# Running the context half of a second block in turns between expert blocks, on one core

## The reference

```
first_block(x):                         # 256 tokens
    h += forgetting_attention(norm(h));  h += hier_moe(norm(h), layer 0)
    h += retention(norm(h));             h += hier_moe(norm(h), layer 1)
hier_moe: 32 experts, top 2 of 8 in one of 4 groups; (silu(a) * b) @ w_down[e], w_gu[e] 1024 x 1024, w_down[e] 512 x 1024
second_block(x, ctx):                   # 256 tokens each, modulated by c and c_ctx
    for each of 2 layers, the same weights for x and ctx:
        p = norm(.) @ w_in              # 1024 x 3088: q, k, v, o, gates, SGU and convolution inputs
        mix = [mlstm (both directions) | spatial gating | depthwise convolution, 31 taps]
        . += gate * (mix @ w_out)       # 1024 x 1024
        . += gate * (silu(n @ w_g) * (n @ w_u)) @ w_down   # 1024 x 5632, 2816 x 1024
```

## Time and profile before

| | us |
|---|---|
| median of three runs | 2858.34 |
| lowest and highest | 2840.27, 2858.52 |
| profiled execution, its time | 2852.59 |
| profiled execution, its span | 2850.8 |

### The profile page before, as it was taken

One profiled execution on the slowest core, in us unless ns is written; L12 is line 12 of the kernel. 1 busy time (PEld: TensorE's weight loads), 2 busy tenths in 40 slices (PEclk: granted clock), 3 DMA queues, 4 the chain that ended last, 5 costly groups with the idle time before them and its releaser, 6 DMA issues. The chain is left out here.

```text
span 2850.8 us, 38893 instructions
## 1 busy us (share of the span) xinstructions
PE 2325.0 (82%) x16840; PEld 1697.3 (60%) x16840; DVE 1020.5 (36%) x1836; ACT 699.5 (25%) x1179; POOL 6.5 (0%) x16
## 2 busy tenths in 40 slices
PE   6998676667779987766666579888999998896998
PEld 6856432323358876423232247676788786675998
DVE  4334410100046354301010166574533226636544
ACT  4422100000034331000000042233322225233442
POOL 0000000000000000000000000000000000000000
PEclk9987778778789998888787788988999999887999
DMA  6473899999965675999999722101232223312542
GB/s 242 158 250 112 336 369 409 386 409 393 409 228 186 214 273 211 382 407 377 409 384 408 288 81 64 55 1 59 89 103 89 82 82 97 99 34 91 189 157 82
DMA packets 239524, 619.65 MB, mean 217 GB/s; under 512 B 11664, under 2 KB 64912, under 8 KB 239216
## 3 DMA queue, kind: packets, MB, share of 16 engines
q1 hardware_dynamic: 238832, 615.56, 57.8%
q0 software_dynamic: 512, 1.48, 0.2%
HBM read 615.95 MB, written 1.05 MB: 216 GB/s over the span
## 5 line engine op out<-in xcount | busy, mean ns | idle before, releaser
L351 PE MATMUL bank<-xh,high 128*128 128x256 f32 (+2 forms) x1328 | 451.5, 340 | 53.6 <-DVE xl L461 35.2
L351 PE MATMUL bank<-xl,high 128*128 128x256 f32 (+2 forms) x1328 | 446.9, 336 | 0.0
L351 PE MATMUL bank<-xh,low 128*128 128x256 f32 (+2 forms) x1328 | 446.3, 336 | 0.0
L351 PEld LDWEIGHTS bank<-xh,high 128*128 128x128 f32 (+1 forms) x1328 | 258.6, 195 | 96.0 <-issue 42.2
L351 PEld LDWEIGHTS bank<-xh,low 128*128 128x128 f32 (+1 forms) x1328 | 258.6, 195 | 25.7 <-issue 1.7
L351 PEld LDWEIGHTS bank<-xl,high 128*128 128x128 f32 (+1 forms) x1328 | 258.9, 195 | 22.6 <-issue 0.5
L1093 DVE TENSOR_TENSOR hs<-hs,bank 64x256 f32<-64x256 f32 x64 | 27.0, 423 | 624.9 <-ACT hs L1088 624.8
L1088 ACT ACTIVATE hs<-bank 64x256 f32<-64x256 f32 x64 | 24.2, 377 | 831.7 <-PE bank L1076 831.7
L318 DVE TENSOR_TENSOR low<-ring__6,high 128x1024 fp32r<-128x1024 f32 (+1 forms) x81 | 94.6, 1174 | 157.2 <-ACT high L309 157.2
L318 DVE TENSOR_TENSOR low<-ring__7,high 128x1024 fp32r<-128x1024 f32 x78 | 95.0, 1224 | 135.0 <-ACT high L309 134.8
L318 DVE TENSOR_TENSOR low<-ring__8,high 128x1024 fp32r<-128x1024 f32 x75 | 91.0, 1224 | 115.9 <-ACT high L309 115.8
(11 more groups left out here) (512 smaller groups left out, 3842.2 us busy)
## 6 DMA issues: line engine op xcount, KB each, us to landing
ring__7<-in_expert_w_down SPq DMA_DIRECT2D x32, 1024.0 KB, 14.4
ring__49<-in_expert_w_gu SPq DMA_DIRECT2D x16, 1024.0 KB, 16.6
ring__50<-in_expert_w_gu SPq DMA_DIRECT2D x16, 1024.0 KB, 18.5
ring__51<-in_expert_w_gu SPq DMA_DIRECT2D x16, 1024.0 KB, 18.5
ring__52<-in_expert_w_gu SPq DMA_DIRECT2D x16, 1024.0 KB, 18.6
ring__53<-in_expert_w_down SPq DMA_DIRECT2D x16, 1024.0 KB, 11.9
ring__54<-in_expert_w_down SPq DMA_DIRECT2D x16, 1024.0 KB, 13.6
ring__8<-in_expert_w_gu SPq DMA_DIRECT2D x16, 1024.0 KB, 15.3
```

Source lines behind the costliest of these rows:

```text
L351: done = pe.matmul(out, a.bitcast(F32R), b.bitcast(F32R), start=kk == 0 and q == 0, stop=stop)
```

## The change

The context half of the second block leaves the tail. Its layer 0 mixer runs inside `moe(0)` (`context_mixer`), its layer 0 FFN and layer 1's keys, values, gates and states inside `moe(1)` (`context_ffn`). Each is a Python generator for every engine. `schedule` takes the next piece of it (a turn) three times in each of its 34 rounds: after `up`, after `across` and after `down`, so 102 turns. The mixer has 72 turns (2 for the norm, 26 projection items, 36 for the scan and what lies around it, 8 output items). The part in `moe(1)` has 105 (2, 44 + 24 FFN items, 2, 10 projection items, 23), and three of them come behind the last round. The tail works on x's 256 columns and begins its scan from saved `states[L]` and `last_m`.

The weights for the turns go through the same ring. One load (up to 1 MB) serves two turns, and is issued two turns ahead of the first. To make room in the on-chip memory, the ring has 6 slots in the expert stages in place of 12, 5 in `fox`, 4 in `ret`, and 8 in the tail in place of 3; GB is 4; three banks serve `prepare`, `across` and `down` in place of four, and the eighth is the turns' own (`Halves`), with one matmul of zeros to open each group. The tables `cos`, `sin` and `dec` (0.79 MB) leave the load of `vec` and come in `ret` by POOL's queue. In the tail DVE does 5 taps after an item.

The core of the diff:

```diff
-GB = 8
+GB = 4
-NSLOT = 12
+NSLOT = 10
+NMOE = 6
...
+            def sp_paced(self, sp):
+
+                ahead = len(self.pairs.items)
+                self.loads(sp, 0, ahead)
+                for it in self.items:
+                    self.loads(sp, it["at"] + ahead, it["at"] + ahead + 1)
+                    yield it
...
+            def act_paced(self, act):
+                ahead = len(self.pairs.items)
+                self.act_high(act, ahead)
+                for it in self.items:
+                    self.evict(act, "a", ev_a, it)
+                    self.act_high(act, it["at"] + ahead + 1)
+                    yield it
...
-        def moe(L, before, opened, early_name, x_ready):
-            room = Room(f"moe{L}", 12, before, opened)
+        def moe(L, before, opened, early_name, x_ready, beside):
+
+            room = Room(f"moe{L}", NMOE, before, opened)
+            room.keeps = MORE[0]
...
+                turns = side["sp"](sp)
+                run(schedule(none, none, up, none, down, none, turns))
+                run(turns)
...
-            def schedule(prepare, scatter, up, across, down, back):
+            def schedule(prepare, scatter, up, across, down, back, turns):
                 prepare(0)
                 for b in range(NE + 2):
                     if b < NE:
                         up(b)
                     if b == 0:
                         scatter(0)
-                    if b % GB == 5 and b // GB + 1 < NE // GB:
+                    next(turns, None)
+                    if b % GB == 2 and b // GB + 1 < NE // GB:
                         prepare(b // GB + 1)
                         scatter(b // GB + 1)
                     if 1 <= b <= NE:
                         across(b - 1)
+                    next(turns, None)
                     if b >= 2:
                         back(b - 2)
                     if 1 <= b <= NE:
                         down(b - 1)
+                    next(turns, None)
                     yield b
...
+            room = Room("ret", 4, before, opened)
...
+        def context_mixer(room, bk):
+            return mixer(0, 0, room, room.part, room, bk, [], 2, 256, 7, 1)[2]
+
+        def context_ffn(room, bk):
+
+            pairs = pair_buffers(room, 2)
+            _, x_done, xx, first = ffn(0, 0, room, bk, [], pairs, 256, lambda c: [])
+            st, get = room.part()
+            second = mixer(1, 0, get, None, room, bk, x_done(7), pairs, 256, 7, 1, x_ready=x_done, xx=xx)[2]
+            st.close()
+            return one_after_another(first, second)
+
+        def x_mixer(L, before, opened, early_in, x_ready):
+            room = Room(f"mix{L}", 8, before, opened)
+            early, x_done, s = mixer(L, 1, room, room.part, room, banks, opened, 4, 512, 5, 2, early_in, x_ready)
```

## The result

The changed kernel takes 2965.57 us, median of four runs (2957.31 to 2983.26); the kernel before takes 2856.24 beside it. The ratio is 1.0403, with a 95% interval of 1.0342 to 1.0465. The forecast was slower, by 2.0% (2913). The time lies inside the range, the direction is right and the forecast step is half of what came. In the profiled executions the spans are 2965.5 and 2850.8, so 114.7 us more, where my sum had 60.

A forecast was written before the change was run, and what follows sets the result against it. Expert stages were taken as bound by transfers and the tail by PE. Turns cost 464 us, the tail and earlier weights give back 404, so +60 on the profiled 2852.6 gives 2913 us, range 2750 to 3010.

The forecast's parts named there:

- What bounds the kernel: Whole kernel: expert stages set by transfers at 394 GB/s with PE some 9 us a block free; the tail the opposite.
- The walk's mechanism: Expert stages: expert loads queue behind late-freed turn slots, PE waits for down and fourth up quarters; two blocks take 47.0 us.
- The tail's -404: Tail: 404 us saved through 256-column FFN, mixers, scans, outputs and norms, and earlier first weights.
- `moe(1)`'s +293: `ret` and `moe(1)`: 293 us more, including 226 for 26.6 blocks at 8.5 each.
- `prepare`: Expert stages, gather for four blocks: half meets free time, so it adds 1.0 us per block.
- `moe(0)`'s +171: Stretch to the end of `moe(0)`: 171 us more, including 70 for taps and 57 for projection and output.
- the taps' 70: `moe(0)`, 14 turns (4.7 blocks): DVE's gate steps or taps behind `low` add 6.4 per block, 70 us with the 8.5.
- The clock: Expert stages: one turn in six at 1.2 GHz, 1.0 us per block over 38 blocks, 38 us.
- The low-clock rival: Expert stages: two turns in three at 1.2 GHz, 114 us more, 3027 in all; chance 0.13.
- The fed stream: Expert stages: each block costs only the 4.5 us of its extra loads, 2666 (2650 to 2720); chance 0.13.
- 15.5 us of PE work: Expert stages: PE's 6.66 plus three turns of 2.95 per block would fit within the 20.5 us of loads.
- The rival with half the stalls: Expert stages: queue restarts, taps and clock cost half, 2787 (2720 to 2830); chance 0.18.

The follow-up runs named there:

- e1: Changed kernel with its six ring slots divided, four for the experts' loads and two for the turns' loads: 2879.94 us, ratio 1.0103 to the kernel before.
- e5: Divided ring, plus the tail's first two high and low copies made ahead of the norm's root and split: 2859.49 us, ratio 1.0038 to the kernel before.
- e9: Changed kernel with its shared six slots, DVE making the one-hot tiles a round earlier: 2914.30 us, ratio 1.0247 to the kernel before.
- e12: Changed kernel with half of prepare's gather matmuls left out (output not the reference's): 2952.82 us, ratio 1.0381 to the kernel before.
- e11: Divided ring, early one-hot tiles, tail's first pairs early, and 4 gate steps or taps per item, not 7: 2798.48 us, ratio 0.9808 to the kernel before.
- small loads: Divided ring with each turn's load an eighth of its size, all engine work kept (output not the reference's): 2841.0 us, one run.
- e10: Changed kernel with divided ring, early one-hot tiles and the tail's first pairs ahead of the norm: 2792.90 us, ratio 0.9814 to the kernel before.
- e6: Divided ring, with DVE making the one-hot tiles of the next four blocks a round earlier: 2814.50 us, ratio 0.9896 to the kernel before.
- e4: Changed kernel without the context part: no turns, x's scan from zero states (output not the reference's): 2469.91 us, ratio 0.8655 to the kernel before.

## Why the prediction was right or wrong

**What bounds the kernel** held: expert stages by transfers, the tail by PE. The walk's mechanism held too. e1 parts the slots and leaves all work and its order; though each user then has fewer slots than before, `ret` and `moe(1)` lose 97 us. The two waits of the walk stand in the timeline at nearly its sizes. What failed are terms of the two sums, and they pulled apart: 36 us in the tail and 33 in `moe(1)` were missing, and `moe(0)` had 15 too many, which hid part of it by luck.

**The tail's -404 was the larger failure**: 368 came, 36 of the 55 us that are missing. The step that failed is the gaps ahead of the first matmuls: "Its norm stretch of 28 us halves", "6 more are in the norm ahead of `ffn(0)`", "now 10 less", and the 7 for `ffn(1)`'s first weights. In the table these four, 36 us, gave nothing. I took the columns to halve the norm's time and passed over that `act_paced` and `dve_paced` make the first pairs behind the norm. e5 shows 20 us of it; no run parts the other 16. The projections, scans, outputs and FFNs together gave what the sum had. The tail is 852 us by the row of the additions, so that it also stood at the border of the sign "if the tail keeps over 850 us"; my 1206 was counted from 13 us later.

**`moe(1)`'s +293 was too low by 33, and that lies at its start.** By the starts of `across`:

| part of `ret` and `moe(1)` | before | changed | more | in the sum |
|---|---|---|---|---|
| `ret` to its last addition | 278.0 | 285.2 | 7 | 2 |
| from there to the sixth `across` | 125.4 | 232.2 | 107 | 74 (five blocks of 9.5, preload 16, norm 10) |
| 16 blocks, four periods | 256.7 | 420.8 | 164 | 152 |
| the rest | 159.8 | 207.8 | 48 | 65 (5.6 blocks, late turns 12) |

Here a step stands that the sum put at nothing. Between two `low` of the first turns DVE has a list of small steps that finds which further blocks the tokens need (`more_blocks`, L1452 to L1476). The slot of the turns' load comes free only behind it, and the first `down` load waits on SP for that slot:

```profile
1317.74 1.22 DVE L378 TENSOR_TENSOR low<-ring__12,high 128x1024 fp32r<-128x1024 f32 x1 [5.69 <-ACT high L369]
1318.88 0.17 DVE L1452 TENSOR_SCALAR nb<-cnt 128x32 f32<-128x32 f32 x1
...
1333.25 0.17 DVE L1476 CAST eid<-ids 1x32 int32<-1x32 f32 x1
...
1333.79 1.21 DVE L378 TENSOR_TENSOR low<-ring__12,high 128x1024 fp32r<-128x1024 f32 x1
```

```profile
1335.04 0.37 SPq L230 DMA_DIRECT2D ring__12<-in_expert_w_down  x1
```

```profile
1340.15 1.94 PE L1241 MATMUL bank<-ring__12,ht 128*32 128x256 f32 x16 [12.83 <-DMA ring__12<-in_expert_w_down]
```

PE waits 12.83 us, and 14.56 at the same place of `moe(0)`; before, the same steps of DVE cost it 5.07 in `moe(1)`. It is the walk's own mechanism, with 15 us of DVE in the place of 2.4. No run moves these steps, so that their share of the 33 isn't shown beyond these waits.

**`prepare`** ("half of it meets free time, so 1.0 per block") was mis-sized too. A period is 105.2 and not 102, 12 us over 16 blocks. It began with a wait of 2.96 on DVE that the rows of before show as 1.72. e9 shows that the waits with what followed them were worth 44 to 52 us in both stages. That `prepare`'s own matmuls are as dear was not shown; e12 gave 6 to 19 for 25 us of them, so that a part of them seems to have met free time.

**`moe(0)`'s +171** became 156. To the tenth `across` it grew by 135, where the sum has 139 with the taps' 70; behind it by 21, where it has 33 for scan, output and clock. That the first part is so near is luck: it holds the 14.56 us that the sum didn't have, and e11 doesn't bear the taps out at 6.4 per block.

**The clock** (38 us, one turn in six at the low level) was near. By the starts of neighbouring matmuls of a turn, 21% of them ran at the low level in `moe(1)`'s stream and 20% in `moe(0)`'s, 51 us in sum. The low-clock rival (two turns in three) fell; over the stream 0.87 was granted, above the 0.79 of before.

**The fed stream** (2666) didn't come: 300 GB/s. Nor did it in any run with the slots parted: with the divided ring the periods stay at 88.0, with small loads at 84.7 and with the three edits at 83.6, above the 4 x 20.5 = 82 of the transfers. My 15.5 us of PE work, which "would fit", was the step that was too low (17 to 18.2). For that step I had drawn on the Trainium skill, page "Trainium Kernel Development and Optimization", section "Performance Expectations", which calls matmul busy time a bad metric for how close a kernel is to roofline, and names the busy share of weight loads as one of the good ones. Whether more work fits is another question, and for that the matmuls' figure was the nearer one here: in e1's window weight loads are busy 227 of 352 us, matmuls 295, and the period shrank by 3 us of 88 when the turns' loads shrank to an eighth.

**The rival with half the stalls** (2787) didn't come for the changed kernel. e10, with three edits, comes to 2793.

## What to carry to other kernels

Where a change moves work under other work, the forecast is the difference of two large sums: make each from steps on the chain and not from halves of windows, look at the first round of a stage by itself, and give the result the error of both. Loads whose slots come free at different times are a bad match for one first-in, first-out ring behind one in-order queue. Here it paid to divide the ring (86 us) and to let the larger user have the rest while the other is silent (28 more). Look for producers that stand one step too late in program order (the one-hot tiles, the first weight pair): moving them ahead was worth 1.6 to 2.1% and 0.65%, while moving the consumer gave nothing.

## What the hardware showed beside

The matmuls behind a wait can cost a second time. The same 32 matmuls took 3.73 us straight behind a turn at full clock (2.4 GHz), and behind a wait of 2.96 us 3.81 in six groups of the changed kernel and 6.61 in another, with 0.55 granted. In e12 16 of them took 2.02 us in four groups of `moe(1)` and 3.75 at 0.50 (1.2 GHz) behind waits of 4.71 and 2.96; yet the group at 1590.71 in the changed kernel ran at 1.00 behind waits of 4.69 and 2.96. What the waits cost behind themselves is read from the sum over the groups, not from one row.

Loads with 1 KB rows are a fifth of the loads in e6's periods, and the DMA engines, 100% busy there, moved 376 GB/s; in e4, where there are none, they moved 402. These two differ in more than the rows, and no run parts them.

```profile
1401.73:1737.08 335.35, 288.66 (x3118) 221.87 (x3118) 95.58 (x138) 70.98 (x117) 0.00 (x0) 0.97 1.00 376
```
